# Gates' sigmoids, the next chunk's first steps and the weights' high parts in another order on ScalarE, in the recurrent layer of a four-layer block

## The chip, the cores and the metric

The kernel runs on one core of one Trainium2 chip. A core has TensorE (PE, with its weight loads PEld), VectorE (DVE), ScalarE (ACT), GpSimd (POOL) and a queue for transfers, SyncE (SP); each runs its own instructions strictly in the order in which they were written, and they meet through semaphores. The metric is the device time in microseconds (us) of one execution; lower is better.

## The reference, cut to what matters

Two blocks of two layers each work on 512 positions of width 1024. The second layer of the first block is the one that changes. Per position t and channel, with 12 heads of 128 channels:

```
xr, gate = split(rmsnorm(h) @ w_in)             # 1536 + 1536 columns
xc = causal_depthwise_conv(xr, conv_w, conv_b)  # 4 taps
r  = sigmoid(xc_head @ w_rg + b_rg)             # per head, 128 x 128
i  = sigmoid(xc_head @ w_ig + b_ig)
log_a = -8 * r * softplus(-lam);  a = exp(log_a)
b  = sqrt(-expm1(2 * log_a)) * (i * xc)
hs[t] = a[t] * hs[t-1] + b[t]                   # scan over the positions
out = h + (hs * silu(gate)) @ w_out
```

The other layers (a convolution with pooling, a state space mixer, attention with a window, two MLPs) aren't touched.

## The kernel before

Channels lie on the 128 partitions and positions along the free axis, so a chunk of 128 channels is a tile of 128 x 512. Everything is float32, and every product is made of three matmuls: weights and inputs are split into a high part (rounded to what TensorE multiplies exactly, float32r) and a low part, and high x high, low x high and high x low are added in one PSUM bank. A weight unit is 128 x 1024. SP fetches it into `RAW`, ScalarE copies its high part into `WH` (`high`, L284), GpSimd subtracts for the low part `WL` (`low`, L288). There are three buffers of each, and `WH` of a unit may be written once the unit three before it is multiplied.

The layer is a list of units, `ODD`, that TensorE goes through in this order:

```
X0 X1 X2 X3 X4 R0 X5 ... X11 R1 G0 ... G5 R2 G6 ... G11 O0 ... O7 Q0 ... Q3
```

X is a chunk of the convolution's branch, G a chunk of the gate branch, R the gates r and i of four heads (R0 of heads 0 to 3), O and Q the output. X, G and O take 24 matmuls of 512 columns (L312), R takes 8 products of three matmuls (L295 to L297), one product per r or i of a head. These 8 products share two PSUM banks in turn, so the product for r of a head can start only when ScalarE has read r of the head before it (`act_gates`, L934, and L939 for i).

Around a unit X the other engines do this, for chunk h: DVE scales the bank into `XP` (L418); ScalarE makes the first tap of the convolution in the bank (L905, `B<-XP,VE`), DVE adds the three other taps (L992), ScalarE copies the high part into `Yh` (L421, `act_parts`), DVE subtracts for the low part `Yl` (L425), GpSimd adds both to `XC` (L1076). For G the first step is ScalarE's Silu in the bank (L909), then DVE multiplies by the scan's result (L997), and `Yh`, `Yl` follow. In `dve_odd` the taps of chunk h stand behind the scaling of chunk h+1. `worked(n)` and `parted(n)` name the chunks whose later steps and whose split stand at unit n.

After an R, ScalarE has three runs over four heads, each with its own table of functions: Tanh (L915), Sqrt (L890), Exp (L967, two heads at once and two later). DVE then has `lru_input` (L1043, L1046, L1048) and the scan (L1053), GpSimd two products (L1064, L1081).

What ScalarE does is written by `act_odd`, unit by unit. The order of each engine is fixed by this code; nothing is reordered later. Line 922 is a one-element activation whose only effect is to load the table of Sigmoid early, behind X2 and X9.

Of the kernel before, what the change touches and what calls it, by code (L numbers as in the profile page):

```python
# [12 lines left out]
ACT = mybir.ActivationFunctionType  # L13
AX = mybir.AxisListType

T = 512
# [14 lines left out]
VCOL = {}  # L31
_at = 0
for _n, _c in VECS:
# [15 lines left out]
ODD = ("X0 X1 X2 X3 X4 R0 X5 X6 X7 X8 X9 X10 X11 R1 G0 G1 G2 G3 G4 G5 R2 G6 G7 G8 G9 G10 G11 "  # L49
       "O0 O1 O2 O3 O4 O5 O6 O7 Q0 Q1 Q2 Q3").split()  # L50
EVEN = [(x[0], int(x[1:])) for x in EVEN]
ODD = [(x[0], int(x[1:])) for x in ODD]
# [37 lines left out]
IDX = {what: i for i, what in enumerate(ORDER)}  # L90
assert len(IDX) == len(ORDER) == 281

GLU0 = IDX["glu", 0, 8]
# [4 lines left out]
class Signals:  # L98
# [12 lines left out]
    def inc(self, name, key, by=1):  # L111
        s = self.sem(name)
        self.count[name] += by
        assert (name, key) not in self.value, (name, key)
        self.value[name, key] = self.count[name]
        return s, by

    def at(self, name, key):
        s = self.sem(name)
        assert self.known is None or (name, key) in self.known, (name, key)  # L120
        return s, self.known[name, key] if self.known else 1
# [20 lines left out]
def program(nc, ctx, known, D):  # L142
    m = Signals(nc, ctx, known)
    inc, at = m.inc, m.at

    def sb(name, shape, dt=F32, c=ctx):
        return c.enter_context(nc.sbuf_tensor(name, shape, dt))
# [7 lines left out]
    VE = sb("VE", [128, NV])  # L155
# [48 lines left out]
    XP = sb("XP", [128, 2, 3 + T], F32, scope)  # L204
# [16 lines left out]
    X = PX[:, 0:4, :, :, :].rearrange("p (z a) b g c -> p z (a b) g c", z=2)  # L221
# [30 lines left out]
    def vec(name, c):  # L252
        return VE[:, VCOL[name] + c:VCOL[name] + c + 1]
# [15 lines left out]
    def highs(act, end):  # L269

        while upto["hi"] < min(end, len(ORDER)):
            high(act, upto["hi"])
            upto["hi"] += 1
# [6 lines left out]
    def high(act, i):  # L280
        act.wait_ge(*at(f"w_raw{i % NR}", i))
        if i >= NS:
            act.wait_ge(*at("unit", ORDER[i - NS]))
        act.activation(WH[:, i % NS, :], RAW[:, i % NR, :], ACT.Copy).then_inc(*inc("w_hi", i))  # L284
# [122 lines left out]
    def rs(k):  # L407
        return RS[:, NORMS.index(k) % 2, :]

    def stat_copy(act, k):  # L410
        act.wait_ge(*at("stat_spread", k))
        act.activation(rs(k), banks.bank["spread", k][:, :], ACT.Copy).then_inc(*inc("rs", ("spread", k)))
# [7 lines left out]
    def split_hi(act, k, c, dst, src, scale=1.0):  # L420
        act.activation(dst, src, ACT.Copy, scale=scale).then_inc(*inc("x_hi", (k, c)))  # L421
# [355 lines left out]
    def odd_what(n):  # L777
        return ODD_UNIT[ODD[n][0]](ODD[n][1])
# [50 lines left out]
    def lru_t(h):  # L829
        return tmp(2 + h % 4)  # L830

    def lru_s(h):
        return tmp((0, 1, 6, 7)[h % 4])
# [4 lines left out]
    def xs_of(c):  # L838

        return [] if c == 0 else [0, 1] if c == 1 else [c]  # L840

    def kind_at(n):
        return ODD[n][0] if 0 <= n < len(ODD) else ""
# [2 lines left out]


    def worked(n):
        out = [n - 1] if kind_at(n) != "R" else []
        if kind_at(n + 1) == "R":  # L850
            out.append(n)
        return [ODD[i] for i in out if kind_at(i) and kind_at(i) in "XG"]

    def parted(n):
        out = [n - 2, n - 1] if kind_at(n) == "R" else [n - 1] if kind_at(n + 1) != "R" else []
        return [ODD[i] for i in out if kind_at(i) and kind_at(i) in "XG"]

    def own_bank(kind, c):
        return banks.bank[ODD_UNIT[kind](c)][:, :]
# [5 lines left out]
    def gates_at(n):  # L865

        return [(ODD[n - d][1], d) for d in range(1, 6) if 0 <= n - d < len(ODD) and ODD[n - d][0] == "R"]

    def pair(r, second):
        return [4 * r + 2 * second, 4 * r + 2 * second + 1]  # L870

    def late(n):

        return [(s, n - s) for s in (3, 2, 1) if 0 <= n - s < len(ODD) and ODD[n - s][0] in "OQ"]

    def act_odd(act):
        for n in range(len(ODD) + 3):
            for s, i in late(n):
                act_last(act, i, s)
            if n >= len(ODD):  # L880
                continue
            kind, c = ODD[n]
            what = odd_what(n)
            for r, d in gates_at(n):
                if d == 1:
                    for h in pair(r, 0) + pair(r, 1):
                        act.wait_ge(*at("lru_tanh", h))
                        if h > 3:
                            act.wait_ge(*at("lru_r", h - 4))
                        act.activation(lru_s(h), lru_t(h), ACT.Sqrt).then_inc(*inc("lru_sqrt", h))  # L890
                if d in (1, 3):
                    for h in pair(r, d == 3):
                        lru_exp(act, h)
            if kind == "R":
                act_gates(act, pair(c, 0))
                act_parts(act, n)
                act_gates(act, pair(c, 1))
            highs(act, min(IDX[what] + 4, GLU0))
            if kind == "X":
                if c == 1:  # L900
                    stat_copy(act, "odd")
                for h in xs_of(c):
                    act.wait_ge(*at("xp", h))
                    w = VE[:, VCOL["conv_c_w"] + 4 * h:VCOL["conv_c_w"] + 4 * h + 1]
                    act.activation(own_bank("X", h), XP[:, h % 2, 0:T], ACT.Identity, bias=vec("conv_c_b", h),  # L905
                                   scale=w).then_inc(*inc("xc0", h))
            elif kind == "G":
                act.wait_ge(*at("g_x", c))
                act.activation(own_bank("G", c), own_bank("G", c), ACT.Silu).then_inc(*inc("g_silu", c))  # L909
            if kind == "R":  # L910
                for h in pair(c, 0) + pair(c, 1):
                    act.wait_ge(*at("evac_a", ("r", h)))
                    if h > 3:
                        act.wait_ge(*at("scan", h - 4))
                    act.activation(lru_t(h), GT[:, h % 4, :], ACT.Tanh, scale=SP4[:, 0, h:h + 1]).then_inc(*inc("lru_tanh", h))  # L915
            else:
                act_parts(act, n)
            if kind in "OQ":
                act_last(act, n, 0)
            elif (kind, c) in (("X", 2), ("X", 9)):  # L920

                act.activation(SM[:, 12 + c % 2:13 + c % 2], SM2[:, 0:1], ACT.Sigmoid)

    def act_parts(act, n):
        for kind, h in parted(n):
            act.wait_ge(*at("xc" if kind == "X" else "g_y", h))
            split_hi(act, "xc" if kind == "X" else "y", h, Yh[:, h, :], own_bank(kind, h))

    def act_gates(act, heads):
        for h in heads:  # L930
            act.wait_ge(*at("unit", unit_key_ri("r", h)))
            if h > 3:
                act.wait_ge(*at("lru_exp", h - 4))
            act.activation(GT[:, h % 4, :], banks.bank["r", h][:, :], ACT.Sigmoid,  # L934
                           bias=vec("b_rg", h)).then_inc(*inc("evac_a", ("r", h)))
            act.wait_ge(*at("unit", unit_key_ri("i", h)))
            if h > 7:
                act.wait_ge(*at("g_y", h - 8))
            act.activation(IX[:, h % 8, :], banks.bank["i", h][:, :], ACT.Sigmoid,  # L939
                           bias=vec("b_ig", h)).then_inc(*inc("evac_a", ("i", h)))  # L940

    def act_last(act, n, s):
        kind, c = ODD[n]
        if kind == "O" and s == 1:
            act_turns(act, c)
            if c in PX_AT:
                act_px_zero(act, PX_AT[c])
        elif kind == "O" and s == 3:
            if c in PX_AT:
                act_pad(act, "px", PX_AT[c])  # L950
        elif kind == "Q" and s == 0:
            for i in (2 * c, 2 * c + 1):
                act.wait_ge(*at("h", ("q4", i)))
                if i > 3:
                    act.wait_ge(*at("sq_mm", i - 4))
                act.activation(sq_buf(i), H[:, i, :], ACT.Square).then_inc(*inc("sq", ("final", i)))
            if c == 0:
                act_b(act)
            elif c == 3:
                act_pad(act, "ca", 0)  # L960

    def lru_exp(act, h):
        if h < 2:
            act.wait_ge(*at("x_lo", ("ya", 6 + h)))
        else:
            act.wait_ge(*at("scan", h - 2))
        act.activation(lru_e(h), GT[:, h % 4, :], ACT.Exp, scale=SP4[:, 1, h:h + 1]).then_inc(*inc("lru_exp", h))  # L967
# [1693 lines left out]
```

## Time and profile before

| | us |
|---|---|
| median of three timed runs | 1858.98 (1856.68 to 1861.77) |
| the profiled execution | 1854.97 |
| its span, first to last instruction | 1853.2 |

Of the span TensorE is busy 95% (its mean granted clock is 0.972 of full), GpSimd 53%, VectorE 49%, ScalarE 41%. The profiled execution lasts 1.8 us longer than its span, and is 4.0 us under the median of the timed ones. Of the layer in question the units R0, R1 and R2 run from 394.1, 440.4 and 484.1 us of the span; the first Q starts at 572.6 us.

### The profile page before, as it was taken

To read this page: it belongs to the slowest core of one execution; us is meant where nothing else is said; L and a number is where in the kernel's file an instruction comes from. 1 tells how busy PE (TensorE), PEld (TensorE's weight loads), DVE (VectorE), ACT (ScalarE), POOL (GpSimd) and SP (SyncE) were. 2 spreads that over 40 slices of the span, in tenths; PEclk is the share of its full clock that TensorE was granted. 3 is DMA by queue.
4 is the path that set the end of the run, shared out by engine and by line. 5 is a ranking of instruction groups with operands and counts; after the bars stand their busy time and mean duration, and the time that the engine had idled before them with its cause. 6 is when DMAs were issued, how large, how long until landed. Compare 5 with 4: busy or idle time off the path is not lost.

```text
span 1853.2 us, 20888 instructions
## 1 busy us (share of the span) xinstructions
PE 1759.0 (95%) x7994; PEld 1432.1 (77%) x7994; DVE 912.2 (49%) x1305; ACT 761.6 (41%) x1194; POOL 981.5 (53%) x613
## 2 busy tenths in 40 slices
PE   9999988999998888999999999989999999999996
PEld 7887866777787777888888888867567788888885
DVE  3999974847686684642212122555655221212135
ACT  5233324366856564343322223433565341323242
POOL 5868543557656373664444445555436544444462
PEclk9999998999998899999999999989999999999998
DMA  4323222222222123323232323222111223232321
GB/s 162 107 83 107 98 84 81 88 72 92 87 96 68 47 92 103 114 91 103 91 102 92 102 91 102 80 69 91 35 34 59 98 94 102 92 102 92 102 92 46
DMA packets 55107, 164.04 MB, mean 89 GB/s; under 512 B 6368, under 2 KB 14176, under 8 KB 54880
## 3 DMA queue, kind: packets, MB, share of 16 engines
q1 hardware_dynamic: 55008, 162.71, 26.2%
q8 instruction: 64, 1.05, 0.2%
q14 instruction: 35, 0.29, 0.0%
HBM read 156.66 MB, written 6.03 MB: 88 GB/s over the span
## 4 chain that ended last, share of the span: by engine, by line
PE 70%; DVE 12%; ACT 6%; POOL 6%; issue 5%; DMA 0%; SPq 0%; DVEq 0%; POOLq 0%; ACTq 0%
PE B L312 57%; DVE B L595 3%; POOL WL L288 2%; PE B L2177 1%; ACT WH L284 1%; PE B L2088 1%; DVE P0l L429 1%; PE B L295 1%; PE B L1624 1%; PE B L296 1%; PE B L297 1%; PE B L1517 1%; POOL ACC L365 1%; PE B L2159 1%; DVE SW L1121 1%
## 5 line engine op out<-in xcount | busy, mean ns | idle before, releaser
L288 POOL TENSOR_TENSOR WL<-RAW,WH 128x1024 fp32r<-128x1024 f32 x281 | 684.0, 2437 | 634.0 <-ACT WH L284 634.0
L284 ACT ACTIVATE WH<-RAW 128x1024 fp32r<-128x1024 f32 x281 | 297.0, 1059 | 713.2 <-PE B L312 680.8
L312 PE MATMUL B<-P0h,WH 128*128 128x512 f32 x1104 | 433.2, 392 | 5.7 <-ACT P0h L421 4.0
L312 PE MATMUL B<-P0l,WH 128*128 128x512 f32 x1104 | 426.5, 392 | 1.0 <-DVE P0l L429 1.0
L312 PE MATMUL B<-P0h,WL 128*128 128x512 f32 x1104 | 280.6, 391 | 2.3 <-POOL WL L288 2.3
L312 PEld LDWEIGHTS B<-P0h,WH 128*128 128x128 f32 x1104 | 207.7, 188 | 51.4 <-ACT P0h L421 5.1
L312 PEld LDWEIGHTS B<-P0h,WL 128*128 128x128 f32 x1104 | 208.5, 189 | 46.0 <-POOL WL L288 2.7
L312 PEld LDWEIGHTS B<-P0l,WH 128*128 128x128 f32 x1104 | 208.4, 189 | 45.4 <-DVE P0l L429 1.5
L436 DVE TENSOR_TENSOR H<-H,B 128x512 f32<-128x512 f32 x88 | 60.3, 686 | 284.3 <-PE B L312 284.3
L312 PE MATMUL B<-P1h,WH 128*128 128x512 f32 x448 | 174.7, 390 | 0.0
L1897 DVE SCALAR_TENSOR_TENSOR TMP<-B,RS 128x512 f32<-128x512 f32 x64 | 44.1, 691 | 258.4 <-PE B L312 244.0
L312 PE MATMUL B<-P1l,WH 128*128 128x512 f32 x448 | 169.8, 389 | 0.0
L595 DVE SCALAR_TENSOR_TENSOR B<-UP,VE,B 128x512 f32<-128x512 f32 x232 | 156.5, 752 | 1.6 <-ACT B L539 1.6
L312 PE MATMUL B<-P1h,WL 128*128 128x512 f32 x448 | 115.2, 389 | 0.0
L365 POOL TENSOR_TENSOR ACC<-ACC,TMP 128x512 f32<-128x512 f32 x51 | 75.2, 1475 | 53.1 <-ACT TMP L356 52.6
L312 PEld LDWEIGHTS B<-P1h,WL 128*128 128x128 f32 x448 | 84.1, 188 | 17.5
L312 PEld LDWEIGHTS B<-P1l,WH 128*128 128x128 f32 x448 | 84.1, 188 | 17.4
L312 PEld LDWEIGHTS B<-P1h,WH 128*128 128x128 f32 x448 | 84.1, 188 | 17.4
L312 PE MATMUL B<-P2h,WH 128*128 128x512 f32 x144 | 58.0, 402 | 8.5 <-ACT P2h L421 8.5
L2142 POOL TENSOR_SCALAR TMP<-TMP,AS 128x256 f32<-128x256 f32 (+1 forms) x64 | 29.4, 478 | 52.2 <-DVE AS L2136 52.2
L429 DVE SCALAR_TENSOR_TENSOR P0l<-H,VE,P0h 128x512 fp32r<-128x512 f32 x40 | 48.4, 1223 | 13.5 <-ACT P0h L421 13.5
L312 PE MATMUL B<-P2l,WH 128*128 128x512 f32 x144 | 55.0, 407 | 0.0
(346 smaller groups left out, 2828.0 us busy)
## 6 DMA issues: line engine op xcount, KB each, us to landing
RAW<-in_w SPq DMA_DIRECT2D x281, 512.0 KB, 3.2
H<-in_xT SPq DMA_DIRECT2D x8, 256.0 KB, 4.7
g<-GB SPq DMA_DIRECT2D x8, 256.0 KB, 2.1
GB<-g SPq DMA_DIRECT2D x32, 64.0 KB, 2.0
out<-TMP SPq DMA_DIRECT2D x8, 256.0 KB, 2.2
u<-TMP SPq DMA_DIRECT2D x7, 256.0 KB, 2.0
U<-u SPq DMA_DIRECT2D x28, 64.0 KB, 2.0
SPT<-in_ssm SPq DMA_DIRECT2D x1, 1040.0 KB, 5.7
```

The source lines that it names most:

```text
L284: act.activation(WH[:, i % NS, :], RAW[:, i % NR, :], ACT.Copy).then_inc(*inc("w_hi", i))
L288: pool.tensor_tensor(WL[:, i % NS, :], RAW[:, i % NR, :], WH[:, i % NS, :].bitcast(F32), ALU.subtract).then_inc(*inc("w_lo", i))
L295: pe.matmul(out, wh, xh, start=start, stop=False)
L296: pe.matmul(out, wl, xh, start=False, stop=False)
L297: return pe.matmul(out, wh, xl, start=False, stop=stop)
L312: return pe.matmul(b[:, :], w[:, ws[c]], x[:, c, :], start=start, stop=stop)
L365: pool.tensor_tensor(ACC[:, :], ACC[:, :], tmp(c % 2), ALU.add).then_inc(*inc("acc", (k, c)))
L429: dve.scalar_tensor_tensor(dst, src, g, hi.bitcast(F32), ALU.mult, ALU.subtract).then_inc(*inc("x_lo", (k, c)))
L436: dve.tensor_tensor(H[:, n, :], H[:, n, :], banks.bank[what][:, :], ALU.add).then_inc(*inc("h", key))
L595: dve.scalar_tensor_tensor(chunk(c) if j == 30 else CB[c % 2][:, :], UP[:, c, j:j + T], w, CB[c % 2][:, :], ALU.mult, ALU.add).then_inc(*i ...
L1897: dve.scalar_tensor_tensor(mlp_tmp(q, c), banks.bank[what][:, :], 0.0, rs(f"mlp{l}"), ALU.max, ALU.mult).then_inc(*inc("evac_d", what))
L2142: pool.tensor_scalar(s_head(n, h), s_head(n, h), st[:, 16 + h:17 + h], 1.0, ALU.mult, ALU.mult).then_inc(*inc("att_w", (n, h)))
```

## The change

`worked(n)` and `parted(n)` now both give just the chunk before, at every unit. Before, the two chunks ahead of an R were split together, both between the first and the second pair of the gates. The first step of a chunk (first tap or Silu) moves into a function of its own, `act_first`, and at an R it now stands between the pairs (X) or behind both pairs (G). The high part of the weights that stood at the unit ahead of an R now stands behind the gates. A Sigmoid preload is added behind G5.

```diff
     def worked(n):
-        out = [n - 1] if kind_at(n) != "R" else []
-        if kind_at(n + 1) == "R":
-            out.append(n)
-        return [ODD[i] for i in out if kind_at(i) and kind_at(i) in "XG"]
-
-    def parted(n):
-        out = [n - 2, n - 1] if kind_at(n) == "R" else [n - 1] if kind_at(n + 1) != "R" else []
-        return [ODD[i] for i in out if kind_at(i) and kind_at(i) in "XG"]
+        return [ODD[n - 1]] if kind_at(n - 1) and kind_at(n - 1) in "XG" else []
+
+    parted = worked
@@ act_odd
             if kind == "R":
                 act_gates(act, pair(c, 0))
+                if kind_at(n - 1) == "X":
+                    act_first(act, n - 1)
+                act_gates(act, pair(c, 1))
+                if kind_at(n - 1) == "G":
+                    act_first(act, n - 1)
+                highs(act, IDX[what] + 3)
                 act_parts(act, n)
-                act_gates(act, pair(c, 1))
-            highs(act, min(IDX[what] + 4, GLU0))
-            if kind == "X":
...
-            elif kind == "G":
...
+                highs(act, IDX[what] + 4)
+            elif kind_at(n + 1) != "R":
+                highs(act, min(IDX[what] + 4, GLU0))
+                act_first(act, n)
@@
-            elif (kind, c) in (("X", 2), ("X", 9)):
+            elif (kind, c) in (("X", 2), ("X", 9), ("G", 5)):
 
                 act.activation(SM[:, 12 + c % 2:13 + c % 2], SM2[:, 0:1], ACT.Sigmoid)
```

`act_first` holds the two branches that were here (the first tap with `stat_copy` at X1, and the Silu), unchanged. The call `act_parts(act, n)` for units that aren't R stays where it was, at the end of the unit.

ScalarE's queue at R0, before (from the high part of the weights ahead of the first gate, `GT` is r and `IX` is i, `B<-XP,VE` the first tap, `Yh<-B` a chunk's high part):

```order
L421 ACTIVATE Yh<-B 128x512
L284 ACTIVATE WH<-RAW 128x1024
L905 ACTIVATE B<-XP,VE 128x512
L934 ACTIVATE GT<-B,VE 128x512
L939 ACTIVATE IX<-B,VE 128x512
L934 ACTIVATE GT<-B,VE 128x512
L939 ACTIVATE IX<-B,VE 128x512
L421 ACTIVATE Yh<-B 128x512 x2
L934 ACTIVATE GT<-B,VE 128x512
L939 ACTIVATE IX<-B,VE 128x512
```

and now (line numbers are those of the changed file, where 924 is the first tap, 940 and 945 the gates):

```order
L421 ACTIVATE Yh<-B 128x512 x2
L940 ACTIVATE GT<-B,VE 128x512
L945 ACTIVATE IX<-B,VE 128x512
L940 ACTIVATE GT<-B,VE 128x512
L945 ACTIVATE IX<-B,VE 128x512
L924 ACTIVATE B<-XP,VE 128x512
L940 ACTIVATE GT<-B,VE 128x512
L945 ACTIVATE IX<-B,VE 128x512
L940 ACTIVATE GT<-B,VE 128x512
L945 ACTIVATE IX<-B,VE 128x512
L284 ACTIVATE WH<-RAW 128x1024
L421 ACTIVATE Yh<-B 128x512
```

The first tap of X4 and a high part of weights have left the place ahead of the first gate, and the split of X3 (the second of the two `Yh<-B` at the top) has come there. R1 reads the same, with X11 and X10.

ScalarE's queue at R2, before (L909 is Silu):

```order
L284 ACTIVATE WH<-RAW 128x1024
L909 ACTIVATE B<-B 128x512
L934 ACT_TABLE_LOAD
L934 ACTIVATE GT<-B,VE 128x512
L939 ACTIVATE IX<-B,VE 128x512
L934 ACTIVATE GT<-B,VE 128x512
L939 ACTIVATE IX<-B,VE 128x512
L421 ACTIVATE Yh<-B 128x512 x2
```

and now, from the split of G3 and G4 to the high part behind the gates (L914 is the preload, L928 Silu):

```order
L421 ACTIVATE Yh<-B 128x512 x2
L914 ACT_TABLE_LOAD
L914 ACTIVATE SM<-SM 128x1
L940 ACTIVATE GT<-B,VE 128x512
L945 ACTIVATE IX<-B,VE 128x512
L940 ACTIVATE GT<-B,VE 128x512
L945 ACTIVATE IX<-B,VE 128x512
L940 ACTIVATE GT<-B,VE 128x512
L945 ACTIVATE IX<-B,VE 128x512
L940 ACTIVATE GT<-B,VE 128x512
```

The load of Sigmoid's table stands behind the split of G4, and Silu of G5 with a further table load follows the last gate. TensorE's and SP's orders are unchanged; on DVE one split `Yl` moves ahead of three taps at R0 and at R1, and on GpSimd one sum `XC` moves ahead of the products that follow R0 and R1.

## Rows read from the trace of the kernel before

**Rows 1.** The page's first line, and who TensorE waited for, 340 to 572 us.

```profile
span 1853.2 us, 20888 instructions
PE B L295 <- ACT GT L934: 8.6, 7, 3.3
```

**Rows 2.** Timeline of TensorE at R0: start, duration, instruction, [idle before <-releaser].

```profile
395.22 0.39 PE L297 MATMUL B<-Yl,WH 128*128 128x512 f32 x1
396.83 0.47 PE L295 MATMUL B<-Yh,WH 128*128 128x512 f32 x1 [1.22 <-ACT GT L934]
402.35 0.39 PE L312 MATMUL B<-P0h,WH 128*128 128x512 f32 x1
```

**Rows 3.** Timeline of VectorE at R0.

```profile
394.34 0.69 DVE L418 TENSOR_TENSOR XP<-B,RS 128x512 f32<-128x512 f32 x1 [1.14 <-PE B L312]
394.95 4.57 DVE L992 SCALAR_TENSOR_TENSOR B<-XP,VE,B 128x512 f32<-128x512 f32 x6
```

**Rows 4.** Timeline of ScalarE at R0.

```profile
394.35 1.06 ACT L284 ACTIVATE WH<-RAW 128x1024 fp32r<-128x1024 f32 x1 [1.87 <-PE B L312]
395.31 0.76 ACT L905 ACTIVATE B<-XP,VE 128x512 f32<-128x512 f32 x1
396.02 0.67 ACT L934 ACTIVATE GT<-B,VE 128x512 f32<-128x512 f32 x1
...
397.80 0.69 ACT L934 ACTIVATE GT<-B,VE 128x512 f32<-128x512 f32 x1 [0.54 <-PE B L297]
...
399.09 1.08 ACT L421 ACTIVATE Yh<-B 128x512 fp32r<-128x512 f32 x2
400.05 0.69 ACT L934 ACTIVATE GT<-B,VE 128x512 f32<-128x512 f32 x1
...
404.08 2.56 ACT L915 ACTIVATE TMP<-GT,SP 128x512 f32<-128x512 f32 x4
```

**Rows 5.** Timeline of VectorE from R0's Exp to R1, first and last row.

```profile
412.19 0.69 DVE L1043 SCALAR_TENSOR_TENSOR TMP<-B,TMP 128x512 f32<-128x512 f32 x1 [3.46 <-ACT B L967]
...
443.05 0.68 DVE L418 TENSOR_TENSOR XP<-B,RS 128x512 f32<-128x512 f32 x1
```

**Rows 6.** Stretches: busy time (instructions) of each engine, PEclk, DMA share, GB/s.

```profile
412.19:443.05 30.86, 29.76 (x132) 24.31 (x130) 29.43 (x42) 17.27 (x23) 25.70 (x18) 1.00 0.25 86
503.40:546.89 43.49, 43.49 (x194) 36.01 (x193) 41.66 (x52) 24.74 (x33) 24.43 (x14) 1.00 0.29 98
446.40:449.40 3.00, 3.00 (x9) 2.09 (x7) 2.47 (x5) 2.48 (x5) 1.21 (x1) 0.50 0.49 175
```

**Rows 7.** Timeline of ScalarE, the first gate of R1.

```profile
444.49 0.67 ACT L934 ACTIVATE GT<-B,VE 128x512 f32<-128x512 f32 x1
```

**Rows 8.** Timeline of TensorE: first wait of R1, end of R1, first wait of R2, start of Q0.

```profile
445.30 0.47 PE L295 MATMUL B<-Yh,WH 128*128 128x512 f32 x1 [3.35 <-ACT GT L934]
...
451.45 0.40 PE L312 MATMUL B<-P0h,WH 128*128 128x512 f32 x1
...
488.07 0.47 PE L295 MATMUL B<-Yh,WH 128*128 128x512 f32 x1 [2.43 <-ACT GT L934]
...
572.62 0.79 PE L295 MATMUL B<-Yh,WH 128*128 128x512 f32 x1 [2.74 <-POOL WL L288]
```

**Rows 9.** Timeline of VectorE ahead of R2: a scan, the scaling and the product.

```profile
468.49 2.33 DVE L1053 TENSOR_TENSOR_SCAN IX<-TMP,B 128x512 f32<-128x512 f32 x2 [1.78 <-POOL TMP L1081]
...
484.32 0.70 DVE L418 TENSOR_TENSOR B<-B,RS 128x512 f32<-128x512 f32 x1 [0.65 <-PE B L312]
484.93 0.69 DVE L997 TENSOR_TENSOR B<-B,IX 128x512 f32<-128x512 f32 x1
```

**Rows 10.** Timeline of ScalarE at R2.

```profile
485.35 0.58 ACT L909 ACTIVATE B<-B 128x512 f32<-128x512 f32 x1
485.94 1.28 ACT L934 ACT_TABLE_LOAD   x1
487.24 0.69 ACT L934 ACTIVATE GT<-B,VE 128x512 f32<-128x512 f32 x1
```

More of the change, by code:

```diff
@@ L895, in act_odd @@
                 act_gates(act, pair(c, 0))
-                act_parts(act, n)
-                act_gates(act, pair(c, 1))
-            highs(act, min(IDX[what] + 4, GLU0))
-            if kind == "X":
[L900 to L906, printed above, removed]
-            elif kind == "G":
-                act.wait_ge(*at("g_x", c))
-                act.activation(own_bank("G", c), own_bank("G", c), ACT.Silu).then_inc(*inc("g_silu", c))
+                if kind_at(n - 1) == "X":
[4 more added lines that the diff above has]
+                highs(act, IDX[what] + 3)
+                act_parts(act, n)
+                highs(act, IDX[what] + 4)
+            elif kind_at(n + 1) != "R":
+                highs(act, min(IDX[what] + 4, GLU0))
+                act_first(act, n)
             if kind == "R":
@@ L919, in act_odd, with act_first @@
                 act_last(act, n, 0)
-            elif (kind, c) in (("X", 2), ("X", 9)):
+            elif (kind, c) in (("X", 2), ("X", 9), ("G", 5)):
                 act.activation(SM[:, 12 + c % 2:13 + c % 2], SM2[:, 0:1], ACT.Sigmoid)
+    def act_first(act, n):
+        kind, c = ODD[n]
+        if kind == "X":
+            if c == 1:
+                stat_copy(act, "odd")
+            for h in xs_of(c):
+                act.wait_ge(*at("xp", h))
+                w = VE[:, VCOL["conv_c_w"] + 4 * h:VCOL["conv_c_w"] + 4 * h + 1]
+                act.activation(own_bank("X", h), XP[:, h % 2, 0:T], ACT.Identity, bias=vec("conv_c_b", h),
+                               scale=w).then_inc(*inc("xc0", h))
+        elif kind == "G":
+            act.wait_ge(*at("g_x", c))
+            act.activation(own_bank("G", c), own_bank("G", c), ACT.Silu).then_inc(*inc("g_silu", c))
     def act_parts(act, n):
```

## The prediction, made before the changed kernel ran

> **What bounds the kernel now.** I read the page first: over the whole span TensorE is busy nearly all the time, so an edit on ScalarE counts only where TensorE waits for it. The waits of TensorE from 340 to 572 us then show the place: 8.6 us in 7 waits for the gates' evacuation, the longest 3.3 us [rows 1]. The timeline of TensorE at R0 shows what one such wait is: after the first two products it stops until the first gate is read from its bank, resumes at 396.83, and reaches X5 at 402.35 [rows 2]. At R1 and R2 the same wait is 3.35 and 2.43 us [rows 8]. Then I read who is late at that point. ScalarE at R0 does the weights' high part and the first tap of X4 ahead of the first gate, and gets to the gate at 396.02 [rows 4]. The timelines of VectorE and the chain of waits told the rest: from the first Exp behind R0 to R1, VectorE is busy 29.43 of 30.86 us, and again 41.66 of 43.49 us behind R2 [rows 6]. In these two stretches no instruction of VectorE waits for TensorE; they begin with a wait for ScalarE's Exp [rows 5]. The second one runs on through the O units to the wait of 2.74 us in front of Q0 [rows 8]. So two things set the end: when the gates are read, and when ScalarE is through with the gates and starts Tanh, Sqrt and Exp.
>
> **The change, part by part.**
>
> *Ahead of the first gate, R0.* Two instructions go, from 394.35 to 396.02, 1.67 us together [rows 4]. But the order shows that the split of X3 comes there, and this is what I think decides. The split needs the three taps of X3, which VectorE makes behind the scaling of X4, and that scaling waits for TensorE's unit X4 until 394.34 [rows 3]. Six taps take 4.57 us from 394.95, so the third ends near 394.95 + 2.29 = 397.24 [rows 3]. A split holds ScalarE for (400.05 - 399.09) / 2 = 0.48 us [rows 4], so the first gate starts near 397.8 instead of 396.02: +1.8 us. TensorE waits behind it, in order, and nothing else can be sent. Before, the same split stood behind the first pair and found its data ready.
>
> *Between the pairs, R0.* The step from the second head's gate to the third's was 400.05 - 397.80 = 2.25 us with two splits in it [rows 4]. Now the gates of the second head end at 399.09 - 397.80 = 1.29 us after their start, and the first tap adds 396.02 - 395.31 = 0.71: 2.00 us, a gain of 0.25. TensorE's end of R0 is then 1.8 - 0.25 = 1.55 us later.
>
> *Behind the gates, R0.* A high part stood there; now two high parts and a split do. A high part holds ScalarE 395.31 - 394.35 = 0.96 us [rows 4], so Tanh moves by another 0.96 + 0.48 = 1.44. Together 1.8 - 0.25 + 1.44 = +3.0 us for Tanh, and since Tanh to Exp follow without waits, for VectorE's row at 412.19 [rows 5].
>
> *The clock.* TensorE's wait at R0 was 1.22 us [rows 2] and becomes 3.0. Behind the wait of 3.35 the granted clock was 0.50 in a stretch of 3 us [rows 6], which is the lower of its two levels, 1.2 of 2.4 GHz; behind 2.74 the first matmul took 0.79 us, behind 2.43 it took 0.47 as at the full clock [rows 8]. So I expect the drop at R0. Its price is the difference between the two stages: 451.45 - 445.30 = 6.15 against 402.35 - 396.83 = 5.52, 0.6 us [rows 2, 8]. Its bounds are 0, if the clock holds, and twice 0.6, if it stays low for the whole stage.
>
> *R1.* The Exp is 3.0 + 0.6 = 3.6 us late, and VectorE's full stretch [rows 6] passes that on to the scaling of X11, at 443.05 before [rows 5]. From that scaling to the first gate it was 444.49 - 443.05 = 1.44 [rows 5, 7]. Now the split of X10 is ahead of the gate, so it is the scaling (394.95 - 394.34 = 0.61), three taps (2.29) and the split (0.48) [rows 3, 4]: 3.4 us, 2.0 more. First gate of R1: +5.6. TensorE's end of R1: +5.6 - 0.25 = +5.35; Tanh: +5.6 - 0.25 + 1.44 = +6.8. The drop of the clock is in the rows of before already. TensorE will wait about 6 us here.
>
> *R1 to R2.* One sum on GpSimd, of about 1.3 us, has moved away from before the scan at 468.49, which waited 1.78 us for GpSimd [rows 9]. So VectorE is +5.5 there. At 484.32 it waited 0.65 us for TensorE [rows 9]; TensorE's +5.35 decides.
>
> *R2.* The split of G4 needs the product that ends at 484.93 + 0.69 = 485.62 [rows 9], +5.35 = 490.97. Behind it come the split (0.48), the table load (487.24 - 485.94 = 1.30 [rows 10]) and a one-element activation (about 0.1): the gate starts near 492.9, +5.7 against 487.24. The preload hides nothing, since it stands behind the late split. Between the pairs nothing is left, and the step goes from about 2.2 to 1.8 us, -0.4. Behind the gates there are now a table load (1.30), Silu (0.6), two high parts and a split: against one high part, 1.30 + 0.58 + 0.96 + 0.48 = 3.3 more. Tanh: 5.7 - 0.4 + 3.3 = +8.6. The wait of 2.43 becomes about 2.8, between the one that left the clock up and the one that didn't; half of 0.6 for it.
>
> *From there on.* VectorE's second full stretch and the chain through ScalarE and GpSimd carry the delay to Q0 [rows 6, 8]. The slack of the banks is used up (O0 will wait for the split of G8), but that lies beside it. What the high parts behind the gates delay for the weights costs nothing itself: the unit that needs them comes one or two units later, each (440.4 - 402.35) / 7 = 5.4 us [rows 2]. If that cover were gone TensorE would wait for `WH` in X6, which I don't expect. Sum: 8.6 + 0.3 = 8.9, rounded to +9 us, of which the two clock terms are 0.9. On the profiled execution's 1854.97 that gives 1864 us; on the median of the timed runs, 1858.98, it gives 1868. The latter is my forecast, since the median lies 4.0 above the profiled one.
>
> The price of a table load is one place where page and trace differ. The row shows 1.28 us for the load and the next activation 1.30 us after its start, with no gap ahead of it [rows 10]. By the Trainium skill, "ScalarE: Activation LUTs", section "What ACT_TABLE_LOAD costs", a switch is 1283 ns and a drain of about 1380 ns. With the page's price for the one load that is added, Tanh behind R2 would be another 1.4 us late and the sum 10.3 us; I stay with the row.
>
> **The rivals.**
>
> *Gates really first, faster.* If the split's data were there at the start of R, each R would gain the 1.67 us ahead of its first gate and 0.25 to 0.4 between the pairs, about 2 us each. With the tail behind the gates hidden, the three give 3 to 6 us: 1853 to 1856. For it speaks that all the waits of R0 to R2 are for the gates [rows 1]. Against it speaks VectorE's row: the taps can't start before 394.95 [rows 3].
>
> *Absorbed, no change that can be told.* The delays of the first gates are real, but each stage's tail is hidden: +1.55 at R0, 2.0 - 0.25 at R1, and 0.35 - 0.4 at R2, +3.3 in all, 1862. It holds if VectorE's stretches have slack that I don't see. Its busy shares of 95 and 96% [rows 6] leave 1.4 and 1.8 us.
>
> *A longer low clock.* The wait of some 6 us in front of R1's second head is nearly twice that of before. If the lower clock lasts through R1 and into G0, TensorE loses another 3 to 5 us: 1872. Only the row of 3.00 us speaks for the length of such a stretch [rows 6], after a wait half as long.
>
> **How the numbers follow.** What a measurement of this kernel can tell from no change is about 0.3%, 5.6 us, so the border is at 1864.6. The forecast has 0.62, the longer low clock 0.10, the absorbed case 0.19, the faster one 0.09. Nearly all of the first two is slower by over 0.3% (0.70); the rest of them with the absorbed case makes 0.21 for no change; faster 0.09. The likeliest case's own range is 1864 to 1871: without the two clock terms it is 8.0 less 1 for a measurement, and on the other side twice the clock's price. For 8 in 10 it goes down to 1860, to take in most of the absorbed case, and up to 1874.
>
> **What would show it.** In the changed kernel's timeline ScalarE's first gate of R0 should start near 397.8, waiting behind `Yh` for VectorE's taps; TensorE's wait there should be 3 us instead of 1.22. Tanh should start near 407 to 408. At R1 TensorE should wait about 6 us, and the scaling of X11 should be at 446 to 447. TensorE's total wait for the gates should go from 8.6 to some 14 us, a wait for `Yl` should show at O0, and Q0 should start near 581. Wrong it would be if the first gate of R0 came before 396, or if the first gate of R1 were late by less than 3 us, since then VectorE's stretch has the slack that I deny it.

## The result and the profile after

| | before | changed |
|---|---|---|
| median of the timed runs, us | 1856.68 (1853.51 to 1861.77, 7 runs) | 1865.46 (1861.42 to 1871.26, 7 runs) |
| ratio | | 1.0048, 95% interval 1.003 to 1.0066 |
| profiled execution, its span, us | 1854.97, 1853.2 | 1861.42, 1859.6 |

The changed kernel is 0.48% slower, 8.8 us between the medians. The spans of the two profiled executions differ by 6.4 us only, and the reason lies ahead of the changed code, where both programs are the same. Here are two stretches of the first layer in the kernel before, and then in the changed one; behind the stretch and its length, the columns are busy time (instructions) of PE, PEld, DVE, ACT, POOL, then the granted clock, DMA share and GB/s:

```profile
160.00:180.00 20.00, 17.69 (x71) 14.20 (x70) 20.00 (x32) 7.48 (x10) 19.54 (x14) 0.91 0.23 79
300.00:320.00 20.00, 13.10 (x39) 8.51 (x38) 15.79 (x26) 10.26 (x16) 3.85 (x2) 0.74 0.29 106
```

```profile
160.00:180.00 20.00, 18.09 (x80) 14.66 (x79) 20.00 (x32) 7.48 (x10) 19.54 (x14) 1.00 0.27 83
300.00:320.00 20.00, 12.61 (x41) 8.36 (x40) 14.95 (x23) 11.62 (x18) 4.19 (x2) 0.83 0.26 102
```

In this execution of the changed kernel TensorE spent 20.5 us at the low clock before R0, in that of the kernel before 27.3 us (sums of the low stretches in the two traces). At half speed that is 3.4 us of the 3.65 by which R0 began earlier, at 390.44 us instead of 394.09. The code is the same there, so this is luck. In the 14 profiles of this document R0 begins anywhere between 389.6 and 394.1 us. So all comparisons below count from TensorE's first product of R0, to the start of Q0, and to the first square sums (the matmuls `B<-MG,TMP` behind Q1), where the delay from this layer has passed through all engines. Before, those square sums start 589.68 - 394.09 = 195.6 us after R0's first product; changed, 595.89 - 390.44 = 205.45: 9.9 us later. Where two kernels have the same code up to an event, numbers counted in this way repeat to 0.01 to 0.2 us, as the table of the experiments shows (before and e2 at R0 and R1; changed, e3 and e9).

TensorE, ScalarE and VectorE of the changed kernel at R0 (start, duration, instruction), to be held against [rows 2 to 4]:

```profile
390.44 0.39 PE L295 MATMUL B<-Yh,WH 128*128 128x512 f32 x1
...
394.99 0.76 PE L295 MATMUL B<-Yh,WH 128*128 128x512 f32 x1 [3.02 <-DVE Yl L425]
395.55 0.63 PE L296 MATMUL B<-Yh,WL 128*128 128x512 f32 x1
...
401.48 0.39 PE L312 MATMUL B<-P0h,WH 128*128 128x512 f32 x1
```

```profile
393.67 0.60 ACT L421 ACTIVATE Yh<-B 128x512 fp32r<-128x512 f32 x1 [4.84 <-DVE B L998]
394.16 0.68 ACT L940 ACTIVATE GT<-B,VE 128x512 f32<-128x512 f32 x1
...
404.64 2.55 ACT L907 ACTIVATE TMP<-GT,SP 128x512 f32<-128x512 f32 x4
```

```profile
390.70 0.69 DVE L418 TENSOR_TENSOR XP<-B,RS 128x512 f32<-128x512 f32 x1 [1.15 <-PE B L312]
391.31 2.33 DVE L998 SCALAR_TENSOR_TENSOR B<-XP,VE,B 128x512 f32<-128x512 f32 x3
394.30 0.69 DVE L425 TENSOR_TENSOR Yl<-B,Yh 128x512 fp32r<-128x512 f32 x1 [0.66 <-ACT Yh L421]
```

ScalarE stands idle for 4.84 us with the split of X3 at the head of its queue, until VectorE's three taps end; the gate, whose data was ready long before, comes behind it. Mind the releaser in TensorE's row. It names `Yl`, which happens to end at 394.99, but the product of the second head needs the bank that the gate reads: the gate ends at 394.84 and TensorE resumes 0.15 us later, as it did behind the gate of before (396.69 and 396.83 [rows 2, 4]).

R1 and R2, and what follows, of the changed kernel, against [rows 8]; then stretches of low clock: two of the changed kernel (at R0 and R1), and last the one of the kernel before at R1:

```profile
447.64 0.76 PE L295 MATMUL B<-Yh,WH 128*128 128x512 f32 x1 [5.75 <-DVE Yl L425]
...
491.51 0.47 PE L295 MATMUL B<-Yh,WH 128*128 128x512 f32 x1 [2.84 <-ACT GT L940]
...
531.90 0.50 PE L312 MATMUL B<-Yh,WH 128*128 128x512 f32 x1 [2.49 <-DVE Yl L425]
...
578.88 0.79 PE L295 MATMUL B<-Yh,WH 128*128 128x512 f32 x1 [2.85 <-POOL WL L288]
```

```profile
394.99:397.68 2.69, 2.69 (x6) 2.02 (x7) 0.00 (x1) 1.12 (x2) 0.00 (x0) 0.50 0.00 0
445.72:452.55 6.83, 4.91 (x12) 3.66 (x12) 1.84 (x3) 4.41 (x7) 0.00 (x0) 0.50 0.01 4
```

```profile
446.17:449.58 3.41, 3.41 (x10) 2.22 (x8) 2.88 (x5) 2.80 (x5) 1.44 (x2) 0.50 0.43 154
```

At R1 TensorE multiplies at the low clock for 4.91 us instead of 3.41.

The wait in front of Q0 is as long as before (2.85 against 2.74 us), although TensorE got there 9.9 us later: the whole chain of the other engines has moved by the same amount. This is what a delay that is handed on looks like.

### The profile page after: what moved, and what is told of

Read it like the earlier page. It is cut to its first block, busy times and chain, and to the rows that moved or that the text cites. A ratio compares the mean times of both kernels' runs of the same rounds, so it can differ in the third digit from the quotient of the medians.

```text
span 1859.6 us, 20890 instructions
## 1 busy us (share of the span) xinstructions
PE 1757.9 (95%) x7994; PEld 1430.8 (77%) x7994; DVE 913.4 (49%) x1305; ACT 761.7 (41%) x1196; POOL 980.6 (53%) x613
## 4 chain that ended last, share of the span: by engine, by line
PE 70%; DVE 12%; ACT 6%; POOL 6%; issue 5%; DMA 0%; SPq 0%; DVEq 0%; POOLq 0%; ACTq 0%
PE B L312 57%; DVE B L595 3%; POOL WL L288 2%; PE B L2183 1%; PE B L2094 1%; ACT WH L284 1%; PE B L295 1%; PE B L1630 1%; PE B L296 1%; PE B L297 1%; DVE P0l L429 1%; PE B L1523 1%; DVE B L998 1%; POOL ACC L365 1%; PE B L2165 1%
```

## The experiments

The table has all of them, counted from R0's first product. The profile behind each row is of one execution; the ratio is to the kernel before on the same chip, with its 95% interval.

| kernel | first gate of R0, R1, R2 | Tanh behind R0, R1, R2 | square sums | ratio |
|---|---|---|---|---|
| before | 1.93, 50.40, 93.15 | 9.99, 59.10, 101.20 | 195.6 | |
| changed | 3.72, 56.38, 100.25 | 14.20, 67.21, 111.22 | 205.45 | 1.0048 (1.003 to 1.0066) |
| e1_split_behind | 0.88, 48.65, 88.70 | 10.66, 58.34, 99.65 | 194.0 | 1.0001 (0.9982 to 1.0021) |
| e2_r2_only | 1.93, 50.39, 93.64 | 9.99, 59.18, 104.61 | 198.9 | 1.0017 (0.9999 to 1.0034) |
| e3_r0r1_only | 3.72, 56.40, 100.01 | 14.22, 67.39, 108.06 | 202.4 | 1.0032 (1.0017 to 1.0048) |
| e4_tanh_first | 0.88, 49.67, 90.15 | 8.29, 56.99, 98.74 | 195.4 | 0.9998 (0.9981 to 1.0014) |
| e7_filler | 3.72, 55.12, 97.34 | 12.95, 64.31, 108.32 | 202.6 | 1.0044 (1.0027 to 1.0061) |
| e8_high_behind_gates | 1.71, 51.31, 94.59 | 10.93, 61.58, 104.25 | 198.5 | one run |
| e12_split_ahead | 3.72, 54.97, 98.36 | 12.58, 63.82, 107.08 | 201.3 | one run |
| e9_no_preload | 3.73, 56.41, 100.18 | 14.23, 67.25, 111.17 | 205.5 | one run |
| e5_high_behind_exp | 0.88, 49.02, 90.36 | 9.71, 57.79, 100.36 | 196.7 | 1.0002 (0.9989 to 1.0014) |
| e6_silu_late | 0.88, 49.04, 90.34 | 9.72, 57.81, 97.96 | 194.6 | 1.0002 (0.9987 to 1.0018) |
| e10_high_ahead | 1.22, 48.99, 89.42 | 10.06, 57.81, 100.28 | 194.5 | 0.9995 (0.9978 to 1.0012) |
| e11_silu_late | 1.22, 48.98, 89.41 | 10.05, 57.80, 97.05 | 193.05 | 0.9988 (0.9976 to 1.0000) |

### The split moved behind the first pair

```diff
                 if kind_at(n - 1) == "X":
                     act_first(act, n - 1)
+                act_parts(act, n - 1)
                 act_gates(act, pair(c, 1))
...
-            else:
+            elif kind_at(n + 1) != "R":
                 act_parts(act, n)
```

> The changed kernel, but the split of the chunk before (X3, X10, G4) stands between the pairs of gates instead of ahead of the first gate; all else, the longer tail behind the gates too, as changed. Measured from TensorE's first product of R0 to its first of Q0: 178.5 us before, 188.5 us changed. Theory A (what counts is when Tanh starts behind each R, and the split ahead of the first gate is the cause of the loss): the first gates start 1 us after R0 and R2 begin, TensorE's waits for the gates fall under 3 us in all, but the tail with two high parts and a split keeps Tanh where it was, so the stretch comes to about 178, as before the change. Rival B (TensorE's waits for the gates are what counts, the tail is hidden): 173, the median 5 us under the kernel before. Rival C (the split ahead is harmless, the tail or the clock is the cause): 185 or more.

Measured: Q0 starts at 176.9, the square sums at 194.0. Without its early split the changed kernel is 11.5 us shorter (2.9 of them are the clock's, see below), and in the timed runs it is level with the kernel before. C falls, and 176.9 is much nearer to A's 178 than to B's 173. A wasn't right in everything: TensorE's waits at the three R (the second and the last line below) are 3.5 + 0.9 us and not under 3, and Tanh came 0.8 us earlier than before behind R1 and 1.6 behind R2. Of the time that TensorE saved, part went back at once. The first line of this list of its waits from 370 to 592 us is for the square of the first Q chunk (`TMP`), and that wait was 4.3 us before:

```profile
PE B L1396 <- ACT TMP L963: 5.9, 1, 5.9
PE B L295 <- DVE Yl L425: 3.5, 4, 1.6
PE B L312 <- DVE Yl L425: 3.0, 2, 2.5
PE B L295 <- POOL WL L288: 1.6, 1, 1.6
PE B L295 <- ACT GT L941: 0.9, 5, 0.2
```

### The two places apart

`worked`, `parted` and `act_odd` take the new order only at the R that a G precedes (e2), or that an X precedes (e3). e3 has no preload behind G5 either.

```diff
+    def new(n):
+        return kind_at(n) == "R" and kind_at(n - 1) in "G"      # e3: in "X"
```

> The kernel before with the change at R2 alone (split of G4 ahead of the gates, preload, Silu of G5 and one high part behind them); R0 and R1 as before. Theory A: first gate of R2 +0.3 us, Tanh +3.2 to 3.5, and the stretch from R0 to Q0 182, 3.5 over before. Rival B: the tail is hidden, 178.5 to 179. If the parts add up, this and the version with R0 and R1 alone make the 10.0 us of the whole.

> The kernel before with the change at R0 and R1 alone; R2 as before. Theory A: TensorE reaches R2 some 6.7 us later than before as it did in the changed kernel, R2 adds nothing, the stretch from R0 to Q0 is about 185. Rival B, that each stage's delay is local and absorbed: 182 or less.

Measured at Q0: 181.8 and 185.3, as theory A has it. At the square sums they add 3.3 and 6.8 us, 10.1 together, against 9.9 of the whole. The parts add up to within 0.2 us.

### The high part and the split, each alone in the kernel before

```diff
-            highs(act, min(IDX[what] + 4, GLU0))                # e8
+            if kind_at(n + 1) != "R":
+                highs(act, min(IDX[what] + 4, GLU0))
...
             if kind == "R":                                     # e12
+                act_parts(act, n, 0)
                 act_gates(act, pair(c, 0))
-                act_parts(act, n)
+                act_parts(act, n, 1)
```

> The kernel before, and only the weights' high part that stood ahead of the first gate is moved behind the gates at R0, R1 and R2 (1.0 us each). Chain theory: the first gates start up to 1 us earlier and TensorE waits some 2.5 us less at the three R, but Tanh and Exp stay where they were, so TensorE's square sums in front of Q1's end start at 195.6 us from R0 as before, within 0.5, and the time saved at R turns up as a wait at Q0 and there. Rival (TensorE's waits count): 193.

> The kernel before with one thing added: the split of the chunk before (X3, X10, G4) stands ahead of the first gate; high parts, first steps, table loads and VectorE's order as before. If the split ahead is what costs, the first gate of R0 starts 3.7 us after R0's first product (before 1.9), that of R1 about 5 us later than before. By the parts measured so far, 9.9 us of the whole less 2.9 of the high parts behind the gates: 202.6 us from R0 to the first square sums. By my working, with one split less between the pairs: 200.5. If it is harmless: 195.6, as before.

The first expectation failed, and by a step that I had priced wrongly there. The first gate of R0 came only 0.2 us earlier, and the square sums 2.9 us later. ScalarE at R0 in that kernel:

```profile
392.95 0.78 ACT L906 ACTIVATE B<-XP,VE 128x512 f32<-128x512 f32 x1 [2.59 <-DVE XP L418]
393.68 0.67 ACT L935 ACTIVATE GT<-B,VE 128x512 f32<-128x512 f32 x1
...
401.00 2.00 ACT L284 ACTIVATE WH<-RAW 128x1024 fp32r<-128x1024 f32 x2
```

Without the high part ScalarE waits for `XP`, which the high part had covered. It was nearly free ahead of the gates and costs its full 0.96 us on ScalarE behind them: Tanh behind R0 is 0.94 later, and the first gate of R1 0.91. The 2.9 us at the end are not three times 0.96, though. From R1 to R2 the delay of Tanh (2.48) isn't what is handed on, but TensorE's end of R1 (1.54, of which 0.63 is a drop of the clock that lies worse than before), and at R2 the clock fell in this execution, which it didn't in the kernel before. R2 in e8 and before:

```profile
483.53:493.54 10.01, 7.57 (x25) 5.28 (x24) 3.69 (x6) 7.25 (x11) 0.00 (x0) 0.83 0.14 52
```

```profile
484.12:493.55 9.43, 6.20 (x25) 4.27 (x24) 3.29 (x5) 8.08 (x12) 2.35 (x1) 1.00 0.26 96
```

From the first gate of R2 to its end that made 6.98 us instead of 6.32. So about 1.9 us of the 2.9 are the high part, at R0 and R2, and the rest is the clock in this one execution.

The split ahead alone puts the first gate of R0 where the changed kernel has it, 3.72, and costs 5.7 us, the clock included: it fell at R0, as in the changed kernel, and at R2 (0.67 us), where in the changed kernel it didn't. Together 2.9 + 5.7 = 8.6 of the 9.9, but with the two drops at R2 taken off only 7.3, so 1.3 to 2.6 us of the whole are in neither. What neither has is Silu and its table load behind R2's gates, the second split behind the gates instead of between the pairs, and the longer low clock at R1; no run takes these apart.

### The clock

```diff
                         last.then_inc(*inc("unit", what if (h % 4, j) == (3, 1) else (r, h)))
+                    if h % 4 == 0 and c < 2:
+                        b, before = banks.queue[0]
+                        pe.wait_ge(*at(*before))
+                        for _ in range((12, 25)[c]):
+                            pe.matmul(b[:, :], wh[:, 0:128], Yh[:, h, :], start=True, stop=True)
```

> The changed kernel, and TensorE multiplies during its long waits at R0 and R1: 12 and 25 additional matmuls of 512 columns into the bank that the next unit starts anew, so their result is never used. They are shorter than the waits (2.7 of 3.0 us, 5.7 of 5.75). Clock theory: the clock stays at its upper level, R0 takes from its first product to X5 10.3 instead of 11.0 us, R1 13.0 instead of 14.1, the stretch from R0 to Q0 186.3 instead of 188.4. Rival: if the stage's length is set by ScalarE's gates and not by the clock, all stays at 188.4; if the additional matmuls are in the way, it is longer.

The additional matmuls fit into the wait, and behind them TensorE is at full speed (0.40 us for a matmul that took 0.63 in the changed kernel; the granted clock is 1.00 until the end of R0, and through R1 too):

```profile
394.00 2.88 PE L812 MATMUL B<-Yh,WH 128*128 128x512 f32 x12
397.18 0.47 PE L295 MATMUL B<-Yh,WH 128*128 128x512 f32 x1 [0.30 <-DVE Yl L425]
397.49 0.40 PE L296 MATMUL B<-Yh,WL 128*128 128x512 f32 x1
```

R0 took 9.79 us instead of 11.04 and R1 12.48 instead of 14.12, Q0 started at 185.6 and the square sums at 202.6. So the low clock cost the changed kernel 2.9 us, which is just the sum of the two stages. Not all of it is new: the kernel before has its drop at R1 too, worth some 0.6 (from the first gate to the end it takes 6.96 us at R1 and 6.33 at R0). The timed runs can't tell this: the ratio is 1.0044 where the changed kernel has 1.0048, and both intervals hold both.

### The preload

```diff
-            elif (kind, c) in (("X", 2), ("X", 9), ("G", 5)):
+            elif (kind, c) in (("X", 2), ("X", 9)):
```

> The changed kernel without the preload behind G5: Sigmoid's table is then loaded by the first gate. If the preload hides nothing, since it stands behind the late split, first gate of R2 within 0.2 us of the changed kernel's, 205.4 us from R0 to the first square sums, 0.1 less. If it hides its load: 206.7.

Measured: first gate of R2 at 100.18 against 100.25, square sums 205.5. The added preload hides nothing as placed (one execution, but the two agree to 0.07 us). In e1, where no split stands ahead of it, the same load runs while TensorE is still at G5, and the first gate follows 88.70 - 87.82 = 0.9 us behind R2's first product.

### Tries for something better than both

Tanh ahead of the high parts, and the second high part behind Exp:

```diff
+                [the four Tanh]                                 # e4, on e1
                 highs(act, IDX[what] + 3)
                 act_parts(act, n)
-                highs(act, IDX[what] + 4)                       # e5, on e1
...
-            lows(pool, min(IDX[odd_what(n)] + 4, GLU0))         # e5
+            lows(pool, min(IDX[odd_what(n)] + (3 if kind_at(n) == "R" else 4), GLU0))
```

> As the version with the split between the pairs, and Tanh of the four heads stands directly behind the gates (at R2 behind Silu of G5), ahead of the two high parts and the split. Theory A: Tanh is 2.4 us earlier at each R and the gains of R0 and R1 are handed on by VectorE: stretch from R0 to Q0 about 173.5, the median 5 us under the kernel before. Rival B: no difference from the version without this edit. Rival D (the weights' high parts become late for X6, G1 or G7): TensorE waits for WH or WL there, 1 us or more, and the gain is under 3 us.

> The version with the split between the pairs, and the second of the two high parts behind the gates moved on behind the first two Exp, on GpSimd the low part of the same weights behind the two products. Chain theory: Exp is 1.0 us earlier at each R, two of them are handed on: from R0 to the first square sums 192 us (before 195.6, with the split between the pairs alone 194.0), median 3 us under the kernel before. Rival: the scan waits for GpSimd instead, whose low parts now come together, and nothing is gained against 194.

Both missed: e4 had Q0 at 178.4 where I expected 173.5, e5 the square sums at 196.7 where I expected 192. In e4 Tanh came 2.4 us earlier behind R0 (8.29 against 10.66 in e1), but Sqrt and Exp stayed behind the high parts and the split: Exp starts 18.05 us from R0 on, and 18.04 in e1. What VectorE waits for is Exp, so nothing was gained there. And GpSimd, whose high parts ScalarE started 2.4 us later (10.7 against 8.3 us from R0 on), came late with the products (`TMP L1070`), and R1's first gate was 1.0 us later than in e1:

```profile
410.27 0.69 DVE L1049 SCALAR_TENSOR_TENSOR TMP<-B,TMP 128x512 f32<-128x512 f32 x1 [4.88 <-ACT B L973]
412.02 0.70 DVE L1052 SCALAR_TENSOR_TENSOR B<-B,TMP 128x512 f32<-128x512 f32 x1 [1.05 <-POOL TMP L1070]
```

In e5 the weights came late for three units that TensorE reached in full stride, one of them by 2.9 us (the two others by 1.0), with a drop of the clock behind it. This was a rival that I had written down for e4 and not for e5:

```profile
501.44 0.77 PE L312 MATMUL B<-P0h,WH 128*128 128x512 f32 x1 [2.88 <-ACT WH L284]
```

Silu of G5 behind Exp, with that of G6, and its product and split on VectorE later too (on e5; VectorE's lines are left out below), and then the first high part ahead of the gates again (on e1) without and with the late Silu:

```diff
-                if kind_at(n - 1) == "G":                       # e6, e11
-                    act_first(act, n - 1)
...
+                if kind_at(n - 2) + kind_at(n - 1) == "GR":     # e6, e11, at G6
+                    act_first(act, n - 2)
                 act_first(act, n)
+                if kind_at(n - 2) + kind_at(n - 1) == "GR":
+                    act_parts(act, n - 1)
...
-                highs(act, IDX[what] + 3)                       # e10, e11
...
+            if kind_at(n + 1) == "R":                           # e10, e11, behind the preload
+                highs(act, IDX[what] + 4)
```

> As the version with the high part behind Exp, and behind R2 the Silu of G5 goes together with that of G6, behind Exp, with its product and its split behind lru_input on VectorE. One table load, one Silu and one split leave ScalarE's way to Exp (2.4 us), one product and one split come into VectorE's (1.3 us): 191 us from R0 to the first square sums, 1 us under the version without this edit. Rival: G5's bank or split comes late for G9 and TensorE waits there, no gain.

> The version with the split between the pairs, and the first of the two high parts ahead of the first gate again (at R2 behind the preload). There ScalarE waits for the first product anyway, 0.9 us after R begins, so the gate comes 0.4 us later and what stands behind the gates is 1.0 us shorter: 0.55 us gained at each R, all three handed on: 192.4 us from R0 to the first square sums (194.0 without this edit, 195.6 before), median 3 us under the kernel before. Rival: the gate comes a whole 1.0 us later and nothing is gained.

> As the version with the high part ahead again, and Silu of G5 goes together with that of G6 behind Exp, with G5's product and split behind lru_input. In the pair of versions with the high part behind Exp this edit gave 2.1 us. 190.3 us from R0 to the first square sums, 5.3 under before; median 5 us, 0.28%, under the kernel before. Rival: G5's high part or bank comes late for G9, or VectorE is now what is late for the O units, and 1 us or less is gained over the version without the edit.

The late Silu gave 2.1 us on e5 and 1.5 on e10. All three kernels missed their sums: 194.6 for 191, 194.5 for 192.4 and 193.05 for 190.3. The high part ahead gave 0.6 and 0.5 us for Tanh behind R0 and R1, as expected, but VectorE catches up with TensorE before R2, so only TensorE's end of R1 counts there, and that was 0.36 later. At R2, of the 0.96 us that left ScalarE's way, 0.77 came back as a wait of the next split for VectorE:

```profile
487.12 0.58 ACT L930 ACTIVATE B<-B 128x512 f32<-128x512 f32 x1
488.47 0.60 ACT L421 ACTIVATE Yh<-B 128x512 fp32r<-128x512 f32 x1 [0.77 <-DVE B L1005]
```

e11 is the fastest of all, 2.5 us or 0.14% when counted from R0, and 0.9988 with an interval that reaches 1.0000 in the timed runs. It may be slightly better than the kernel before; that is at the limit of what these runs can tell.

## Why the prediction was right, point by point

The forecast was +9 us and a median of 1868; measured were +8.8 us between the medians, +9.9 counted from R0, and 1865.46. The absolute number lies lower because the median of the kernel before fell from 1858.98 (three runs) to 1856.68 (seven). That +9 came so close has some luck in it: the clock took 1.4 us more than I had for it, and the other terms 0.4 less. And the lower end of the likeliest range, 1864, doesn't follow from its own working: 1858.98 + 8.0 - 1 is 1866, just over what was measured.

Predicted and measured shifts against the kernel before, counted from R0's first product; e7 is the changed kernel with the clock held up at R0 and R1.

| step | predicted | changed | e7 |
|---|---|---|---|
| first gate of R0 | +1.8 | +1.79 | +1.79 |
| TensorE's end of R0 | +1.55, with clock +2.15 | +2.78 | +1.53 |
| Tanh behind R0 | +3.0, with clock +3.6 | +4.21 | +2.96 |
| first gate of R1 | +5.6 | +5.98 | +4.72 |
| Tanh behind R1 | +6.8 | +8.11 | +5.21 |
| TensorE's end of R1 | +5.35 | +6.69 | +3.79 |
| start of R2 | +5.35 | +6.67 | +3.76 |
| first gate of R2 | +5.7 | +7.10 | +4.19 |
| Tanh behind R2 | +8.6, in the sum 8.9 | +10.02 | +7.12 |
| start of Q0 | +9 | +9.9 | +7.0 |

- *The split ahead of the gate.* Right in place at all three R, and in size at R0. At R1 it added 1.8 us (5.98 - 4.21) where I had 2.0, at R2 0.43 (7.10 - 6.67) where I had 0.35. e12 puts it alone into the kernel before and the first gate of R0 is at 3.72, to the hundredth where the changed kernel has it.
- *The tail behind the gates.* Right: between the first gate and Tanh of R0, e7 has 9.23 us, the kernel before 8.06, +1.17 where I had 1.44 - 0.25 = 1.19. At R2, e2 has 10.97 us for it and the kernel before 8.05, +2.92 where I had 3.3 - 0.4 = 2.9. e8 shows the other half at R0: the high part ahead of the gates was covered. Tanh behind Sigmoid or Silu needed no table load in any of these kernels, although the description of the kernel before gives it a table of its own; the sums above have no load for it, which is right.
- *VectorE hands the delay on.* Right from R0 to R1 and from R2 to Q0. From R1 to R2 TensorE's end of R1 decides, as I had it: R2 starts 6.67 us late like that end (6.69), and 1.4 of the 8.11 us of Tanh behind R1 go no further. At the end e2 and e3 make up the whole. The rival "absorbed" is out.
- *The clock.* The mechanism was right and the size was not. I had 0.6 us at R0, nothing new at R1, half of 0.6 at R2. R0 cost 1.25 (2.78 - 1.53), and at R1 TensorE worked at the low clock for 4.9 us instead of 3.4, a part of my third rival, at 1 us (1.64 - 0.6) and not its 3 to 5. At R2 it didn't drop. In all it was 2.9 us, of which the kernel before loses 0.6 too, so 2.3 new ones against my 0.9. The sum of the other terms, 8.0, was then 0.4 too high (7.0 in e7, and 0.6 for the drop at R1 that the kernel before has and e7 has not: 7.6).
- *The table load.* 1.28 us, and the next activation 1.29 us after its start (e9 and the changed kernel alike). The drain that the Trainium skill, "ScalarE: Activation LUTs", section "What ACT_TABLE_LOAD costs", adds to it shows in no row here.
- *TensorE's waits.* I had some 14 us for the three R; it was 8.8 + 3.6 = 12.4. The three long ones were as I had them, 3.02 + 5.75 + 2.84 = 11.6, and the short ones between the other products 0.8 instead of the 1.6 of before. That slow products fill these is likely, but no run shows it.
- *The faster rival.* Its condition, gates really first, is what e1 makes true. It then doesn't give the 3 to 6 us that I priced it with, but 1.6: the tail behind the gates isn't hidden.

## What to carry to other kernels

An in-order queue makes an instruction wait for the data of all that stand ahead of it: when one is moved "behind" something, look at what has come to the front, and at when its data is ready, not at its duration. What stands in a wait is nearly free there and costs its full length on its engine behind it, as the high part did at R0 (0.2 us ahead of the gates, 0.96 behind). And where a chain of other engines sets the end, count what stands ahead of the instruction that the next engine waits for (here Exp), not what the busiest engine waits for; but look at each stage who comes last, for between R1 and R2 that was TensorE.

## What the runs showed of the hardware that was not expected

- A wait doesn't decide alone whether the clock falls. Behind 2.84 us at R2 of the changed kernel the clock stayed at 1.00; behind 2.34 us at R2 of e8 it fell. At one and the same place, in front of Q0, it stayed up behind 2.82 us in e11 and fell behind 2.70 in e3, 2.74 before and 2.85 in the changed kernel.
- The first matmul behind a wait doesn't tell it either, which the prediction took it to do. Behind 3.35 us at R1 of the kernel before it took 0.47 us, and the granted clock fell 0.87 us later; in e8 at R2 it was 0.47 too, and the fall came 0.75 us later.
- The same program loses more or less to the clock from one execution to the next: 0.91 against 1.00 and 0.74 against 0.83 in two stretches of identical code, and 27.3 against 20.5 us at the low clock by the start of R0. Timed runs of the kernel before spread from 1851 to 1866 us over all chips, so a part of 2 us is only seen by counting from a common event in the profile.
- Additional matmuls in a wait of 3 and of 5.75 us (12 and 25 of them) kept TensorE at its full clock in R0 and R1, for 2.9 us less to the square sums by the profile.
